# A two-direction mLSTM scan on one core: gate-sum rows, shared chunk scores and the order inside a step

## The reference, cut to what matters

```python
def step(carry, inp):                       # one chunk of CHUNK = 128 tokens
    C, n, m = carry
    qq, kk, vv, lfc, ii = inp
    b = jnp.cumsum(lfc, axis=-1)
    dmat = jnp.where(lower, b[:, :, None] - b[:, None, :] + ii[:, None, :], -jnp.inf)
    inter = b + m[:, None]
    m_t = jnp.maximum(inter, jnp.max(dmat, axis=-1))
    w_inter = jnp.exp(inter - m_t)
    qk = jnp.einsum('ntd,nsd->nts', qq, kk) * jnp.exp(dmat - m_t[:, :, None])
    num = (w_inter[..., None] * jnp.einsum('nvd,ntd->ntv', C, qq)
           + jnp.einsum('nts,nsv->ntv', qk, vv))
    den = w_inter * jnp.einsum('nd,ntd->nt', n, qq) + qk.sum(-1)
    h = num / jnp.maximum(jnp.abs(den), jnp.exp(-m_t))[..., None]
    ...
    C_new = a[:, None, None] * C + jnp.einsum('ns,nsv,nsd->nvd', w, vv, kk)
```

## Time and profile before

| what | value |
|---|---|
| median of 3 runs | 2144.07 us (2143.94 to 2156.41) |
| profiled execution: span from first to last instruction (the page gives no other time of it) | 2137.7 us |
| PE busy | 2043.5 us, 96% |
| DVE busy | 785.1 us, 37% |
| ACT busy | 406.8 us, 19% |
| mean granted TensorE clock | 0.989 of full speed |
| DMA | 506.73 MB, mean 237 GB/s |

### The profile page before, as it was taken

The page is one execution under the profiler, slowest core; times in us unless marked ns, Lnnn a source line. Parts: engine busy times, 40 slices in busy tenths (PEclk is TensorE's granted clock), DMA queues, the critical chain, the costliest instruction groups (busy, mean ns, idle before and its releaser), DMA issues.

```text
span 2137.7 us, 36835 instructions
## 1 busy us (share of the span) xinstructions
PE 2043.5 (96%) x15858; PEld 1475.7 (69%) x15858; DVE 785.1 (37%) x1780; ACT 406.8 (19%) x964; POOL 5.8 (0%) x12
## 2 busy tenths in 40 slices
PE   8999999999989999999999999998999999999887
PEld 6779999886766666666665666655744667474776
DVE  6737555585431111111111111102426454345454
ACT  1233110103320111000000000001233343123322
POOL 0000000000000000000000000000000000000000
PEclk9999999998999999999999999999999999999999
DMA  9483444545079999999999999996211111131120
GB/s 318 177 273 138 158 177 181 189 165 197 1 302 368 420 419 416 420 420 420 420 418 420 420 420 420 415 420 276 79 59 40 40 40 60 59 118 58 42 80 20
DMA packets 72371, 506.73 MB, mean 237 GB/s; under 512 B 7824, under 2 KB 9872, under 8 KB 11792
## 3 DMA queue, kind: packets, MB, share of 16 engines
q1 hardware_dynamic: 71056, 500.15, 58.5%
q0 software_dynamic: 1152, 4.19, 0.8%
HBM read 503.27 MB, written 1.05 MB: 236 GB/s over the span
## 4 chain that ended last, share of the span: by engine, by line
PE 88%; DMA 5%; DVE 4%; ACT 2%; issue 1%; SPq 0%; DVEq 0%; ACTq 0%
PE ps L451 85%; DMA ring<-weights 3%; DMA work<-weights 2%; PE ps L1189 1%; PE ps L742 1%; DVE work L2658 1%; ACT work L1810 0%; PE ps L618 0%; DVE work L2619 0%; DMA xc<-x_t 0%; DVE work L2725 0%; DVE work L2615 0%; PE ps L1290 0%; DVE work L2616 0%; ACT work L1581 0%
## 5 line engine op out<-in xcount | busy, mean ns | idle before, releaser
L451 PE MATMUL ps<-work 128*32 128x256 f32 (+8 forms) x5608 | 590.2, 383 | 22.3 <-DVE work L2670 6.3
L451 PE MATMUL ps<-work,ring 128*128 128x256 f32 (+2 forms) x2056 | 520.0, 407 | 8.2 <-DVE work L2725 5.0
L451 PEld LDWEIGHTS ps<-work 128*32 128x32 f32 (+3 forms) x5608 | 380.4, 138 | 188.6 <-issue 109.8
L451 PE MATMUL ps<-ring,work 128*32 128x256 f32 (+3 forms) x4824 | 471.3, 413 | 12.6 <-DMA ring<-weights 4.3
L451 PEld LDWEIGHTS ps<-work,ring 128*128 128x128 f32 x2056 | 352.2, 191 | 145.0 <-issue 107.6
L451 PEld LDWEIGHTS ps<-ring,work 128*32 128x32 f32 (+1 forms) x4824 | 260.3, 120 | 148.1 <-issue 78.0
L451 PE MATMUL ps<-xc,ring 128*128 128x256 f32 (+1 forms) x1440 | 278.1, 354 | 5.6 <-DMA ring<-weights 3.9
L451 PEld LDWEIGHTS ps<-xc,ring 128*128 128x128 f32 x1440 | 243.4, 193 | 41.9 <-issue 7.5
L2271 DVE TENSOR_TENSOR work<-work,ps 128x256 f32<-128x256 f32 x42 | 17.7, 421 | 418.7 <-ACT work L1654 418.7
L451 PE MATMUL ps<-xc,work 128*128 128x256 f32 (+1 forms) x720 | 138.3, 351 | 1.0 <-DMA work<-weights 1.0
L451 PEld LDWEIGHTS ps<-xc,work 128*128 128x128 f32 x720 | 120.9, 191 | 20.9 <-DMA work<-weights 4.5
(11 more groups left out here) (276 smaller groups left out, 1179.4 us busy)
## 6 DMA issues: line engine op xcount, KB each, us to landing
ring<-weights SPq DMA_DIRECT2D x317, 1024.0 KB, 11.8
work<-weights SPq DMA_DIRECT2D x154, 1024.0 KB, 16.1
work<-rel POOLq DMA_DIRECT2D x8, 512.0 KB, 9.2
con<-consts SPq DMA_DIRECT2D x1, 1368.0 KB, 21.4
xc<-x_t SPq DMA_DIRECT2D x1, 1024.0 KB, 6.9
xc<-ctx_t SPq DMA_DIRECT2D x1, 1024.0 KB, 24.7
out<-work SPq DMA_DIRECT2D x4, 256.0 KB, 2.1
par<-params SPq DMA_DIRECT2D x1, 872.0 KB, 8.4
```

The costliest lines, as they stand in the source:

```text
L451: ins = eng.matmul(o, lhs, rhs, start=start, stop=stop, **kw)
```

## The change

The gate-sum rows are made by the transpose instruction instead of a matmul with the identity. Between the first two of them a filler is issued. Raw scores are made only in even steps, for the chunks of both directions; ScalarE copies them from PSUM to an SBUF buffer `raw_scores`, and VectorE's `weights` reads them there, in the odd step with the directions exchanged. On TensorE `intra(j, 0)` moves into the piece of the second gate-sum rows, and `state_change(j, 1)` and `intra(j, 1)` become two pieces with a filler between them. On VectorE `state_change(j, 0)` moves ahead of `statistics(j + 1)` and `output(j, 0)` ahead of `state_change(j, 1)`.

```diff
--- before.py
+++ after.py
@@ -295,6 +295,7 @@
         cut = carver(work[:, pre_at:pre_at + 8 * 2 * SEG2], 8 * 2 * SEG2)
         amask, decay = cut(8, P), cut(8, P)
         num, first_inter_s = cut(M_HEADS, M_DH + 1), cut(M_HEADS, M_DH + 1)
+        raw_scores = cut(2, M_HEADS * P)
         cut = carver(work[:, aq_at:aq_at + 2560], 2560)
         k_tok, last_wqk_t = cut(4, M_HEADS * P), cut(M_HEADS, P)
         last_wqk, last_kw = (v.rearrange("p (a b) -> p a b", b=P) for v in (std2, rstd2))
@@ -315,7 +316,7 @@
             late_gates late_row late_row_out late_h late_silu late_weighted late_act late_down late_added
             pre_copied vg_out mv_copied aqk_copied azs_out mzs_out mos_out conv2_acc cqk_out rope_out
             lf_abs lf_ln lf_out cum_out row_masked stats_out stats_exp decay_out
-            qk_weighted qk_turned keys_turned keys_weighted inter_scaled state_out mh_num mh_out
+            scores_kept qk_weighted qk_turned keys_turned keys_weighted inter_scaled state_out mh_num mh_out
             mz_copied mo_copied
             mh_sumsq mh_std mh_normed mh_mixed
             att_scored att_max att_exp att_prob att_turned att_out x_added
@@ -412,12 +413,14 @@
 
         DOWN_READ = {i: ("down_read", n + 1) for n, i in enumerate((6, 7, 5, 2, 4, 3))}
         DOWN_READ[1] = ("snap_out", 4 * UP_PAIRS + 1)
-        ROW = {}
+        KEPT, ROW = {}, {}
         for l in range(DEPTH):
             for j in range(4):
                 for d in range(2):
                     if has_rows(l, j, d):
                         ROW[l, j, d] = len(ROW) + 1
+                        if j % 2 == 0:
+                            KEPT[l, j, d] = len(KEPT) + 1
 
 
         @block.tensor
@@ -1243,7 +1246,7 @@
                     o = fill(("arow", l, j, d), 0, (s["row_masked"], scan_no(l, j, d)))
                     for h in range(M_HEADS):
                         own = cum_a[:, ORDER[d][j], 4 * d + h:4 * d + h + 1].broadcast_to([P, P])
-                        last = mm(o[:, h * P:h * P + P], own, ident, True, True)
+                        last = eng.transpose(o[:, h * P:h * P + P], own, ident)
                     last.then_inc(bank_full[0], 1)
 
                 def inter(j, d):
@@ -1278,7 +1281,7 @@
 
                 def scores(j, d):
                     tok = slice(ORDER[d][j] * P, ORDER[d][j] * P + P)
-                    o = fill(("sc", l, j, d), 3 + d, (s["qk_weighted"], ROW[l, j, d]))
+                    o = fill(("sc", l, j, d), 3 + d, (s["scores_kept"], KEPT[l, j, d]))
                     for h in range(M_HEADS):
                         last = mm(o[:, h * P:h * P + P], cqk[:, h, tok], cqk[:, M_HEADS + h, tok], True, True)
                     last.then_inc(bank_full[3 + d], 1)
@@ -1292,6 +1295,7 @@
 
                 eng.wait_ge(s["cum_out"], l + 2 + l)
                 decay_rows(0, 0)
+                yield
                 decay_rows(0, 1)
                 yield
                 eng.wait_ge(s["cqk_out"], 8 * l + M_HEADS)
@@ -1306,9 +1310,10 @@
                     rows = has_rows(l, j, 0)
                     if l and j == 2:
                         eng.wait_ge(s["mv_copied"], 8 * (l + 1))
-                    if rows:
+                    if rows and j % 2 == 0:
                         scores(j, 0)
                         scores(j, 1)
+                    if rows:
                         inter(j, 0)
                     yield
                     if j < 3:
@@ -1324,12 +1329,12 @@
                     yield
                     if j < 3:
                         decay_rows(j + 1, 1)
-                    yield
                     if rows:
                         intra(j, 0)
                     yield
                     if j < 3:
                         state_change(j, 1)
+                    yield
                     if rows:
                         intra(j, 1)
                     yield
@@ -1339,7 +1344,9 @@
                 total = (32 if l == 0 else 28) - SCAN_START[l]
                 now[0] = -1
                 next(scan)
-                for _ in range(SCAN_START[l]):
+                next(rest)
+                next(scan)
+                for _ in range(SCAN_START[l] - 1):
                     next(rest)
                 for n in range(SCAN_YIELDS):
                     now[0] = n
@@ -1875,6 +1882,15 @@
                         o = tile(eng, "wt", l, j, d)
                         eng.activation(wqk_t[d].rearrange("p a b -> p (a b)"), o, ACT.Copy).then_inc(s["qk_turned"], 1)
 
+                    def keep(d):
+                        o = tile(eng, "sc", l, j, d)
+                        if ROW[l, j, d] > 2:
+                            eng.wait_ge(s["qk_weighted"], ROW[l, j, d] - 1 - 2 * d)
+                        eng.activation(raw_scores[:, d, :], o, ACT.Copy).then_inc(s["scores_kept"], 1)
+
+                    if rows and j % 2 == 0:
+                        keep(0)
+                        keep(1)
                     if rows:
                         inter(0)
                     yield
@@ -2641,7 +2657,9 @@
                     ins.then_inc(s["keys_weighted"], 1)
 
                 def weights(j, d):
-                    o = tile(eng, "sc", l, j, d)
+                    first = j % 2 == 0
+                    o = raw_scores[:, d if first else 1 - d, :]
+                    eng.wait_ge(s["scores_kept"], KEPT[l, j, d] if first else KEPT[l, j - 1, 1 - d])
                     eng.wait_ge(s["decay_out"], ROW[l, j, d])
                     eng.scalar_tensor_tensor(out=wqk[d].rearrange("p a b -> p (a b)"), in0=o, scalar=SC,
                                              in1=decay[:, 4 * d:4 * d + 4, :].rearrange("p a b -> p (a b)"),
@@ -2696,11 +2714,13 @@
                         weights(j, 0)
                         weights(j, 1)
                     if j < 3:
+                        state_change(j, 0)
                         statistics(j + 1)
-                        state_change(j, 0)
+                    if row_work:
+                        output(j, 0)
+                    if j < 3:
                         state_change(j, 1)
                     if row_work:
-                        output(j, 0)
                         output(j, 1)
 
             def mlstm_post(l):
```

## The result

Four runs of the changed kernel took 2113.53 to 2126.52 us, median 2116.0; the kernel before, in the runs taken beside them, 2143.94 to 2156.82, median 2150.24. The ratio is 0.988, 95% interval 0.984 to 0.992: faster by 0.8 to 1.6%. The quotient of the two medians, 0.984, lies at the lower end of that interval, since of the four runs of before two took 2144 us and two over 2156. The forecast was 2115.8. The profiled execution has a span of 2111.4 us and took 2113.53.

The account below looks back on a forecast made before the run. TensorE's own work, 88% of the span, was taken as the bound. Gains of 30.9 us less 2.6 given back, 28.3, took the span from 2137.7 to 2109.4; plus 6.4 gave 2115.8 us, range 2111 to 2124 for 8 in 10.

Parts of the forecast that it names:

- The rows by transposes: Gate-sum rows, both layers: 16 groups of eight matmul records become four transposes, 0.46 us each, 7.4 us gained.
- The scores: Scores made once for two steps: three times sixteen records saved, 5.4 us, less 1.1 for copies in layer 0's step 0.
- The order: New order inside a step: TensorE's waits for VectorE's state and output lines go, 8.2 us in layer 0, 4.8 in layer 1.
- The first filler: Filler between the first two gate-sum rows covers TensorE's wait for their masking, once per layer: 3.1 us gained.
- the filler copies on bank 7: Tile ends move between other pieces, so some TensorE waits for copies out of the filler's bank go: 2.0 us gained.
- The new waits: Layer 0: 1.1 us for the first scaling in step 0, 0.9 to 1.0 for a copy behind the decays in step 1.
- The margin of 0.4 us for the second intra: In a step, the output's first pass is ready at 4.79 us, 0.4 before intra(j, 1) is due at 5.22.
- rival A: Step waits are only exchanged for others: 8.2 + 4.8 comes back, 15.3 us gained, 2128.8 us; chance 0.10.
- 1% is 21.4 us: Whole-kernel verdict: forecast lies 7 us above the 1% bound, so faster but for 0.02; overall faster 0.80, same 0.16, slower 0.04.
- 6.4 above that span: Whole kernel: the runs' median exceeds the traced span by 6.4 us, taken as unchanged and added to 2109.4.
- The span itself: Traced execution of the whole kernel: 2137.7 us before, forecast at 2109.4 after.

Follow-up runs that it names:

- third experiment: The changed kernel with VectorE's old order in a step, TensorE's new order kept: scans 183.3 us against 159.71, ratio to the kernel before 0.997.

## Why the prediction was right, and where it was wrong

**Right, term by term.** The rows by transposes: 7.4 less 0.4 for two short waits forecast, 6.6 net measured. The scores: 5.4 less 1.1, that is 4.3; 4.3 measured. The order: both step waits gone, by VectorE's order alone, 12.1 measured where 8.2 + 4.8 less the filler copy's 0.9 make 12.1. The first filler, 3.1, and the filler copies on bank 7, 2.0, were not taken out alone; the three measured terms leave 5.5 of the 28.5 for these two, and no wait is left between the first rows in either layer. Layer 0 was to win about 15.5 and won 15.8, layer 1 12.5 and 12.75. The new waits stood where they were put: for the first scaling 0.8 idle, for the filler copy 0.9. The margin of 0.4 us for the second intra, the step on which rival A hung, was 0.41.

**Wrong: what can be told.** The step that failed is "1% is 21.4 us, about what this measurement can tell from no change; the forecast lies 7 above that bound and counts as faster but for 0.02". It put the scatter of the runs at next to nothing. The interval of the ratio reaches 0.37%, 7.9 us of 2144, to either side, which is more than those 7. So the measured change of 1.2% is clear of no change, but its interval goes down to 0.8%, under the bound, and a change of over 1% is not shown. The full 28.3 us, 1.32%, with the same scatter would have ended at 0.95%. More runs did not help: six of the changed kernel again have an interval of 0.6 to 1.6%.

The scatter goes with the clock. 36 further runs of the kernel before, taken beside the experiments, went from 2129.60 to 2155.22, nearly in the order of their mean granted clock, 0.994 to 0.981. Compared at the same clock, 0.987 to 0.988, nine runs of before average 2144.4 and five of the changed kernel 2115.0: 29.4 less, near the 28.5 of the scans. This comparison was chosen after the runs were seen.

**Wrong, but hidden: how the sum becomes a time.** "The median of the runs shown lies 6.4 above that span, taken as unchanged" is a step that failed too. The traced execution of before is none of the runs shown. What lies around a span is 2.1 in the changed kernel's profiled execution (2113.53 less 2111.4); the other 4.3 were other executions' clock. After the change the median lay 4.6 above the traced span, so this term was 1.8 too large. The span itself was forecast at 2109.4 and was 2111.4, 2.0 more. It fell by 26.3 and not by the 28.5 of the scans, since 0.7 more passed ahead of layer 0's scan and 1.7 more between the scans, counted from the end of the two fillers behind layer 0's last intra (1796.45 to 1999.69 is 203.24, before 1811.57 to 2013.14 201.57). The latter is a fall of the clock in layer 0's tail. The same 96 records, before and after:

```profile
1830.48 41.47 PE L451 MATMUL ps<-work,ring 128*128 128x512 f32 x96 [3.09 <-DVE work L2725]
1815.36 43.16 PE L454 MATMUL ps<-work,ring 128*128 128x512 f32 x96 [3.09 <-DVE work L2745]
```

and a window over their start after; before, the granted clock is 1.00 there, behind the same wait of 3.09:

```profile
1815.00:1821.00 6.00, 5.64 (x9) 2.41 (x10) 0.51 (x3) 0.00 (x0) 0.00 (x0) 0.72 0.00 0
```

The two errors, 1.8 too much and 2.0 too little, cancel, so that 2115.8 lies within 0.2 of the measured 2116.0 by luck. The saving in the scans, 28.3 forecast and 28.5 measured, is no luck: the transposes, the scores and the order came out as forecast when each was taken alone.

## What to carry to other kernels

When an engine that bounds a stage waits for two results of another engine's queue in each step, look first at the order of that queue: the state update that the next product needed stood behind statistics that nothing needed yet, and moving it, with the output ahead of the second state change, was worth 12.1 us, more than either kind of removed matmul work (6.6 and 4.3). Lay out one step on all queues from the rows, and check each moved instruction against what it now stands behind; copies for other work in the same queue (here ScalarE's filler copies behind the decays) are what is late next. Read a change of 1% from the stage in the trace, and from runs only at the same clock.

## What the runs showed of the hardware

As far as the traces show, the spread of the runs is TensorE's clock outside the scans: the changed kernel's two traces have the same scans within 0.04 us and spans of 2111.4 and 2115.4. In the kernel before the granted clock was 0.69 from 500 to 522 us, a stretch of narrow products (stationary operands of 32 columns, and moving ones of 2), and in the changed kernel 0.70:

```profile
500.00:522.00 22.00, 20.32 (x153) 11.57 (x152) 8.69 (x17) 10.84 (x27) 0.00 (x0) 0.70 0.75 290
```

In the trace with matmul rows this stretch began 4.8 us later, and the same products went through at the upper level, 194 records in 22 us in place of 153:

```profile
505.00:527.00 22.00, 20.32 (x194) 12.60 (x194) 11.43 (x23) 13.05 (x33) 0.00 (x0) 1.00 0.90 349
```

From the first of these products to the next long run of wide ones the changed kernel took 46.69 us (500.19 to 546.88) and the one with matmul rows 37.37 (504.96 to 542.33), 9.3 less, which more than pays for its scans, 6.6 us longer: its one run took 2114.42 us, near the changed kernel's median. Of the eleven traces eight began the stretch between 499.67 and 501.85 us and took 46.65 to 46.73; those that began at 504.96 and 515.32 (VectorE's order alone) took 37.37, and the one that began at 509.03 (TensorE's order alone) 54.74. Where the stretch begins and whether the clock falls go together here; what decides it was not tried.

In the third experiment four of six waits, of 2.47 to 3.36 us, were followed by a fall that cost about 1.7 us on top of the wait, and two, of 2.46, by none. A wait of 3.09 in layer 0's tail was followed by a fall in the changed kernel and by none in the kernel before. So a wait of this length did not settle it by itself. In layer 1's tail, where the changed kernel has a granted clock of 0.81 from 2081 to 2090 us, both kernels with dummies have 1.00 (2081 to 2104 and 2078 to 2098).
